# A dense SwiGLU on two 64-row halves of the TensorE array instead of the whole array

## What is computed

```python
def swiglu(h, w_gate, w_up, w_down):
    return (jax.nn.silu(h @ w_gate) * (h @ w_up)) @ w_down

for layer in range(2):
    h = rms_norm(x, norm_mix_g[layer])
    x = x + (even_mixer if layer == 0 else odd_mixer)(h, ...)
    h = rms_norm(x, norm_ffn_g[layer])
    x = x + (swiglu if layer == 0 else moe_swiglu)(h, ...)   # dense: 1024 -> 3584 -> 1024
return rms_norm(x, norm_final_g)
```

## Time and profile before

| | |
|---|---|
| three timed runs | 1423.88, 1424.10, 1425.11 us |
| median | 1424.1 us |
| span of the profiled execution | 1422.2 us |
| own time of the profiled execution | not among the numbers shown; its span is 1.9 us below the median |
| dense feed-forward in the profile | from 128.97 us to about 362.5 us, 233.5 us |
| TensorE busy in the profile | 1394.8 us, 98% |

### The profile page before, as it was taken

One profiled execution on the slowest core, in us unless ns is written; L12 is line 12 of the kernel. 1 busy time (PEld: TensorE's weight loads), 2 busy tenths in 40 slices (PEclk: granted clock), 3 DMA queues, 4 the chain that ended last, 5 costly groups with the idle time before them and its releaser, 6 DMA issues.

```text
span 1422.2 us, 33237 instructions
## 1 busy us (share of the span) xinstructions
PE 1394.8 (98%) x15137; PEld 833.4 (59%) x15137; DVE 441.0 (31%) x748; ACT 328.8 (23%) x528; POOL 29.7 (2%) x42
## 2 busy tenths in 40 slices
PE   6999999999999999999999999999999999999997
PEld 6987888888899853453453353353354354344344
DVE  4656655655686742101101101101101101101102
ACT  4645545445566531000000000000000000000001
POOL 2000000000012100000000000000000000000000
PEclk9999999999999999999999999999999999999998
DMA  9734555556443489999999999999999999999980
GB/s 296 252 119 146 195 177 194 191 180 198 149 120 140 148 332 326 401 419 389 391 418 387 392 417 389 394 415 393 388 414 400 392 405 402 393 402 408 393 332 32
DMA packets 133041, 438.42 MB, mean 308 GB/s; under 512 B 10690, under 2 KB 64160, under 8 KB 116512
## 3 DMA queue, kind: packets, MB, share of 16 engines
q1 hardware_dynamic: 131824, 433.26, 80.1%
q0 software_dynamic: 1072, 2.98, 0.7%
HBM read 435.16 MB, written 1.05 MB: 307 GB/s over the span
## 4 chain that ended last, share of the span: by engine, by line
PE 95%; DVE 3%; DMA 1%; issue 0%; ACT 0%; POOL 0%; SPq 0%; DVEq 0%
PE bank L1366 41%; PE bank L1387 20%; PE bank L1131 6%; PE bank L881 6%; PE bank L883 6%; PE bank L882 6%; PE bank L1132 4%; PE bank L1134 1%; PE bank L1415 1%; PE bank L1435 1%; DMA raw<-in_ev_w_in 1%; DVE arena L2142 0%; PE bank L1003 0%; PE bank L1049 0%; POOL arena L1849 0%
## 5 line engine op out<-in xcount | busy, mean ns | idle before, releaser
L1366 PE MATMUL bank<-ring,arena 128*32 128x512 f32 (+1 forms) x6144 | 583.5, 540 | 0.0
L1366 PEld LDWEIGHTS bank<-ring,arena 128*32 128x32 f32 x6144 | 197.7, 110 | 365.2 <-issue 362.5
L1387 PE MATMUL bank<-ring,arena 128*32 128x256 f32 x5376 | 291.5, 379 | 0.0
L1387 PEld LDWEIGHTS bank<-ring,arena 128*32 128x32 f32 x5376 | 175.1, 110 | 116.7 <-issue 3.1
L679 DVE TENSOR_TENSOR low<-raw,high 128x2048 fp32r<-128x2048 f32 x73 | 167.3, 2294 | 85.1 <-ACT high L674 84.9
L674 ACT ACTIVATE high<-raw 128x2048 fp32r<-128x2048 f32 x73 | 139.3, 1910 | 55.8 <-PE bank L883 44.1
L1131 PE MATMUL bank<-ht_both,high 128*128 128x512 f32 x392 | 140.5, 398 | 0.6 <-DVE ht_both L1901 0.6
L2413 DVE TENSOR_TENSOR expert_rows<-expert_rows,bank 128x512 f32<-128x512 f32 (+1 forms) x48 | 29.8, 621 | 344.3 <-issue 217.3
L1788 ACT ACTIVATE expert_rows<-bank 128x512 f32<-128x512 f32 (+1 forms) x48 | 25.9, 544 | 422.9 <-PE bank L1366 422.9
L1132 PE MATMUL bank<-ht_both,low 128*128 128x256 f32 x448 | 116.8, 281 | 0.0
L1799 ACT ACTIVATE y_h<-bank 128x256 fp32r<-128x256 f32 x24 | 9.2, 383 | 403.9 <-PE bank L1387 403.9
(11 more groups left out here) (316 smaller groups left out, 1206.8 us busy)
## 6 DMA issues: line engine op xcount, KB each, us to landing
ring<-in_moe_w_down SPq DMA_DIRECT2D x112, 1024.0 KB, 8.4
ring<-in_moe_w_gate SPq DMA_DIRECT2D x64, 1024.0 KB, 9.1
ring<-in_moe_w_up SPq DMA_DIRECT2D x64, 1024.0 KB, 8.6
ring<-in_moe_w_gate SPq DMA_DIRECT2D x64, 768.0 KB, 5.9
ring<-in_moe_w_up SPq DMA_DIRECT2D x64, 768.0 KB, 6.6
raw<-in_ffn_w_gate SPq DMA_DIRECT2D x14, 1024.0 KB, 5.0
raw<-in_ffn_w_up SPq DMA_DIRECT2D x14, 1024.0 KB, 5.0
raw<-in_ffn_w_down SPq DMA_DIRECT2D x14, 1024.0 KB, 5.0
```

Source lines behind the costliest of these rows:

```text
L1366: ins = mm(ps(use)[q * GRP:(q + 1) * GRP, 0:width], rows[:, k, r * GRP:(r + 1) * GRP], weights[:, q, :, :], start=k == 0, stop=k == DK - 1)
L1387: ins = mm(ps(use)[q * GRP:(q + 1) * GRP, 0:DN], m_act_t[:, r, first + c, :], ring[:, at + c * DM + q * DN:at + c * DM + (q + 1) * DN], st ...
```

## The change

The order of pieces becomes g, u of half chunk s, then the down piece of half chunk s - 1 (for s = 1 to 11); the last three down pieces stand at the end. Every matmul of a gate, up or down piece (but the last two down pieces) is cut into two of 64 contraction rows, one on rows 0 to 63 of the array and one on rows 64 to 127, issued one after the other into different banks. A gate or up piece is worked in two phases. In the first, the upper rows go to group 2h and the lower rows to group 2h + 1; in the second they are swapped, so that each bank gets the whole sum. The phases run g, u, g, u, and the second waits for the end of the first of its piece (`tile_step`). All three products go into the same 256 columns of a bank. ScalarE applies Silu directly from the gate bank, VectorE multiplies it with the up bank; the copies of second halves and the additions are gone. A down piece has four turns over pairs of quarters, (0, 2), (1, 3), (2, 0), (3, 1).

```diff
-for _c in range(NCH + 1):
-    if _c < NCH:
-        FFN_ORDER += [("g", _c, 0), ("u", _c, 0), ("g", _c, 1), ("u", _c, 1)]
-    if _c:
-        FFN_ORDER += [("d", _c - 1, 0), ("d", _c - 1, 1)]
+for _s, _half in enumerate(FFN_HALVES):
+    FFN_ORDER += [("g", *_half), ("u", *_half)]
+    if 1 <= _s < len(FFN_HALVES) - 2:
+        FFN_ORDER.append(("d", *FFN_HALVES[_s - 1]))
+FFN_ORDER += [("d", *_half) for _half in FFN_HALVES[-3:]]
...
+            def gate_up_phase(n, second):
+                kind, c, h = FFN_ORDER[n]
+                wh, wl = piece(high, N_FFN + n, DK), piece(low, N_FFN + n, DK)
+                chunks = (2 * h + 1, 2 * h) if second else (2 * h, 2 * h + 1)
+                if not second:
+                    pe.wait_ge(*split_done(N_FFN + n))
+                    for j in chunks:
+                        open_bank(pe, (kind, c, j))
+                else:
+                    tiles.wait(first_phase[n])
+                for k in range(DK):
+                    if n == 0 and not second and k % 2 == 0:
+                        pe.wait_ge(*drained(("norm", 1, k // 2)))
+                    for i, (weights, rows) in enumerate(((wh, ht_h), (wh, ht_l), (wl, ht_h))):
+                        begins, ends = (k, i) == (0, 0), (k, i) == (DK - 1, 2)
+                        for part, j in zip(row_tiles, chunks):
+                            cols = slice((j % 2) * P, (j % 2 + 1) * P)
+                            ins = mm(ps((kind, c, j))[:, 0:SEQ], weights[part, k, cols], rows[part, k, :],
+                                     start=begins and not second, stop=ends and second)
...
+            def ffn_down(n):
...
+                for turn, pair in enumerate(((0, 2), (1, 3), (2, 0), (3, 1))):
+                    if turn > 1:
+                        tiles.wait(marks[turn - 2])
+                    for steps in zip(*(down_products(n, q) for q in pair)):
+                        for part, (q, rows, weights) in zip(row_tiles, steps):
+                            last = mm(ps(("fdown", q)), rows[part], weights[part], start=q not in begun, stop=False)
...
-            def second_halves(kind, c, h):
...
             def silu_pair(c, h):
...
+                    act.wait_ge(*filled(use))
                     if (c, h) != (0, 0):
+                        before = FFN_HALVES[FFN_HALVES.index((c, h)) - 1]
+                        act.wait_ge(*drained(("u", before[0], 2 * before[1] + j % 2)))
+                    fn(f_silu[:, j % 2, :], ps(use)[:, 0:SEQ], ACT.Silu).then_inc(drain_sem(use), 1)
...
-            def gate_sums(c, h):
...
             def gated_pair(c, h):
                 for j in (2 * h, 2 * h + 1):
                     use = ("u", c, j)
+                    dve.wait_ge(*filled(use))
+                    dve.wait_ge(*drained(("g", c, j)))
+                    V.tensor_tensor(f_v[:, j % 2, :], ps(use)[:, 0:SEQ], f_silu[:, j % 2, :],
+                                    ALU.mult).then_inc(drain_sem(use), 1)
...
+            for n in range(SPLITS, FFN_PIECES):
+                kind, c, h = FFN_ORDER[n - SPLITS]
+                if kind == "u":
+                    gated_pair(c, h)
+                low_parts(N_FFN + n)
                 if kind == "u":
                     act_low_pair(c, h)
```

More of the change, by code:

```diff
@@ L1116, in _ @@
             transposes_of_norm(1)
[L1118 to L1136, removed]
@@ L1155, in _ @@
[L1155 to L1159, removed]
-                    last.then_inc(ffn_piece_used, 1)
[L1161 to L1171, removed]
+            tiles = Steps(pe, tile_step)
@@ new lines, in _ @@
+            first_phase = {}
+            def gate_up_phase(n, second):
[17 more added lines that the diff above has]
+                                     start=begins and not second, stop=ends and second)
+                            if ends and second:
+                                ins.then_inc(fill_sem((kind, c, j)), 1)
+                if not second:
+                    first_phase[n] = tiles.mark(ins)
@@ new lines, in down_products @@
+            def down_products(n, q):
+                _, c, h = FFN_ORDER[n]
+                wh, wl = piece(high, N_FFN + n, 2), piece(low, N_FFN + n, 2)
+                t, cols = q // 2, slice(q % 2 * 512, q % 2 * 512 + 512)
+                tokens = slice(t * P, (t + 1) * P)
+                for k in range(2):
+                    a = (c % 2) * 4 + 2 * h + k
+                    for rows, weights in ((f_act_h, wh), (f_act_l, wh), (f_act_h, wl)):
+                        yield q, rows[:, a, tokens], weights[:, k, cols]
@@ new lines, in ffn_down_last @@
+            def ffn_down_last(n, quarters):
+                down_ready(n)
+                for q in quarters:
+                    products = list(down_products(n, q))
+                    for i, (_, rows, weights) in enumerate(products):
+                        last = mm(ps(("fdown", q)), rows, weights, start=False,
+                                  stop=n == FFN_PIECES - 1 and i == len(products) - 1)
+                    if n == FFN_PIECES - 1:
+                        last.then_inc(fill_sem(("fdown", q)), 1)
+                if n == FFN_PIECES - 2 and quarters[-1] == 3:
+                    last.then_inc(ffn_piece_used, 1)
```

94 lines of the change are left out of this document (43 added, 51 removed).

## The result

| | before | changed |
|---|---|---|
| timed runs, median | 1425.08 us (1423.88 to 1426.40, 5 runs) | 1430.0 us (1429.25 to 1432.13, 5 runs) |
| ratio | | 1.0039, 95% interval 1.0027 to 1.0051 |
| span of the profiled execution | 1422.2 us | 1430.3 us |

The changed kernel is slower by 0.4%: 5.6 us by the ratio, 4.9 by the medians. That is the time of rival C of the prediction almost to the microsecond, and the upper end of the range.

The account below looks back on a forecast made before the run. TensorE, busy 98% of the span, was taken as the bound. Gate and up -3.6, down 0, tilings +0.2, waits +1.8 gave -1.6 us: span 1420.6, median 1422.5 us, with 1410.5 to 1430 for 8 in 10.

Parts of the forecast that it names:

- rival C: Gate and up: a full load per 256 columns, 64 rows behaving like 128, 0.120 us a pair, slower, 1429.5 us; chance 21%.
- the likeliest case: Whole kernel: pairs at 0.1148 us plus waits make the stage 1.6 us shorter, 1422.5 us; chance 50%.
- price of a pair: Gate and up: two side-by-side 256-column matmuls on halves take 0.1148 us, 1344 times, 3.6 us less than now.
- down, 288 pairs: Down pieces: pairs of 512 columns on halves keep 0.229 us each, so no change.
- changes of tiling: Stage start and before the last two down pieces: going into another tiling costs about 0.1 us, twice, 0.2 us.
- (a): Stage start: the first up piece is needed at 131.7 but ready at 132.8, so TensorE waits 1.0 us.
- (b): Between half chunks 0 and 1: no down piece covers the Silus, splits and product, so TensorE waits 0.3 to 0.4 us.
- (c): Between half chunks 12 and 13: the same queue of work makes TensorE wait 0.4 us.
- Case B: Gate, up and down: halves stream at or near the clock, 1407.4 us in full, 1413.4 half way; chance 22%.
- Loads behind matmuls: TensorE: by the trace, loads already overlap matmuls on the same rows; only some nanoseconds per load can go.
- D: Every half chunk: Silu, split and product late for the gate by some 0.8 us, 13 times, +10 us, 1433; chance 5%.
- The wait of TensorE on its own first phase: Second phases of gate, up and down: the awaited work ended 2.8 us earlier (down 1.4), so it costs nothing.

Follow-up runs that it names:

- second profile: The changed kernel measured and profiled once more, with nothing altered: 1429.8 us, profiled span 1428.1 us.
- first_whole: The changed kernel with only its first half chunk (gate and up pieces) on the whole array, halves afterwards: 1428.08 us, ratio 1.0031 to the kernel before.
- bench: The changed kernel with 24 settings of test matmuls (tiling, columns, load width) run ahead of the feed-forward: 1538.25 us, only distances between starts read.
- whole_array: The changed kernel with its order and evacuation, but every matmul on all 128 rows, 256 columns per load in gate and up: 1428.04 us, ratio 1.0021.
- three_loads: The kernel before, with each 512-column gate or up matmul cut into two of 256 columns, each with its own load: 1429.34 us, ratio 1.0028.
- grouped: The kernel before, with each group's eight 512-column matmuls first, then its eight of 256: 1422.82 us, ratio 0.9994; repeated, 1423.31 us, 0.9996.
- phases_in_turn: The changed kernel with phases in order g, g, u, u, so each second phase waits for the one directly before: 1438.46 us, ratio 1.010.

## Why the prediction was wrong

Forecast 1422.5, measured 1430.0; the likeliest case had the wrong sign. Of the 7.5 us between them 6.6 are the stage, forecast 1.6 us shorter and measured 5.0 longer; most of the rest is the kernel before, whose median was 1424.1 when I forecast and 1425.08 beside the result. The steps, in its order, with the second profile:

| step | forecast, us | measured, us |
|---|---|---|
| gate, up: price of a pair, 1344 times | 0.1148, -3.6 | 0.120, +3.4 |
| down, 288 pairs | 0.229, 0 | 0.229, 0 |
| changes of tiling | +0.2 | +0.2 |
| (a) start | +1.0 | +1.0, of it 0.7 by another wait (first_whole) |
| (b) half chunks 0 and 1 | +0.4 | +0.14 |
| (c) half chunks 12 and 13 | +0.4 | +0.14 |
| sum | -1.6 | +4.9, stage measured +5.0 |

**The step that failed is the price of a pair.** I took it from `combine` "since `combine` shares the tiling", and reasoned "that a tile hides its load better". The difference, 1344 x 0.0052 = 7.0 us, is more than the 6.6 us by which the stage was missed. bench shows that the tiling is not what sets the price of steps of one width, and whole_array and three_loads that the changed kernel's step costs the same without it. The row that shared the operands, the columns and the product was the right one; that it was for 128 rows did not matter. Its value was in the prediction, as the bad end of the range and as case C, whose price, 0.120, and whose +3.4 came out. That its 1429.5 came out to the half microsecond is partly luck: it held 1.8 us of waits where 1.3 were measured, part of them by another cause, and was counted from a median 1.0 us lower. C got 21%.

The trace of before held a better argument than either row, and I passed over it. 256 columns in 0.120 us and 512 in 0.227 are both 0.013 above their columns at 2.4 GHz (0.107 and 0.213). bench adds 384 columns: 0.173, where the columns alone are 0.160. So at the full clock a matmul of 256 to 512 columns with its load costs **columns / 2.4 GHz plus 13 ns**, and more of them for the same columns must cost more. By this alone 448 more are +6.0 us; it was +3.4, because the alternation of 512 and 256 columns that the change removes had cost 0.353 instead of 0.347, and grouped gets part of that back. How much of the 13 ns is the load and how much the matmul itself is not shown, since no run has one without the other: with 32 or 8 weight columns per load the whole array still took 0.118 and 0.117 in bench, with 8 it took 0.112 in the earlier trace rows. Below 256 columns the form does not hold: bench's first steps of 128 took 0.11 us at the full clock, not 0.067. The Trainium skill, page "TensorE: Matmul & The Clock Gate", section "Back-to-back issue gap", has the same form with 2.5 ns in place of 13, for a matmul without a budget for its load; the runs give 120, 173 and 227 ns, the page's formula 109, 163 and 216. Case B, streaming near the clock, had this small constant for support, and falls.

**Loads behind matmuls.** The prediction weighed the rule of the Trainium skill, page "TensorE: Matmul & The Clock Gate", section "The mechanism", that a load overlaps a running matmul only on another row group, and set the trace against it. The runs side with the trace: with loads on the rows of the running matmul (whole_array) and with loads that could alternate between halves the step is 0.120 us, shorter than one load's record of 0.19.

**The waits.** (a) came out in size and only partly in cause. I followed the split of the up piece and missed that a phase opens two banks, while the second was still the norm's. A step that is moved takes all its waits along, and I did not go through the one in `open_bank`. The wait forecast from 131.7 to 132.8 shrank to 0.3, since the stage began 0.7 late and its steps took 0.120. (b) is seen at 143.56 in the second profile:

```profile
143.38 0.28 PE L1142 MATMUL bank<-ht_both,low 64*128 64x256 f32 x2
143.56 0.50 PE L1142 MATMUL bank<-ht_both,high 64*128 64x256 f32 x4
143.88 0.31 PE L1142 MATMUL bank<-ht_both,low 64*128 64x256 f32 x2
```

0.06 and 0.08 us over the pace. Both (b) and (c) have the forecast place and a third of the size. D did not happen: no other phase is late, and the forecast price of a down step, 0.229, held. The wait of TensorE on its own first phase costs nothing at a distance of 2.88 us, and about 0.3 us at none, as phases_in_turn shows.

**Copies and additions**: nothing gained, as forecast; 40.5 us less work on two engines that nobody waited for. The change of tiling is 0.20 us instead of 0.1, but the first one is not extra: the kernel before too lost about 0.1 in its first step after the transposes, so the sum of 0.2 held.

What the experiments point to is the kernel before with the matmuls grouped, 1.0 us shorter in its profiles and not told from the kernel before by its medians. A version that beats it was not found.

## What to carry to other kernels

Count matmuls and their loads as well as columns. When TensorE is the bound, a change that keeps the columns and cuts them into more matmuls, each with its load, pays for each (here 0.240 us for two of 256 columns, 0.227 for one of 512), and one that widens the matmul behind a load earns it back. Price an unseen form by the row that shares its operand widths, and not by the one that shares its tiling or its look; if two rows disagree and nothing explains why, give the case that each stands for its share. And when a step is moved or doubled, go through every semaphore that it waits for, the opening of a bank too.

## What the hardware showed that was not expected

- **Steps of 128 moving columns were no faster than steps of 256.** At a granted clock of 0.50 (1.2 GHz), steps of only 128 moving columns took 0.213 us (first row of bench above), exactly as long as 256 columns. 128 columns at 1.2 GHz are 0.107. At the full clock, in bench's first steps, they took 0.11 us, against 0.120 for 256. That the load of 128 weight columns sets this pace is my reading and not shown: no setting had 128 moving columns behind a smaller load.
- **At half clock the 13 ns are gone.** 256 columns took 0.213 us in bench and in the earlier trace rows, the columns alone; at full clock 0.120, not 0.107. The full clock gives 1.78 times the pace, not 2.
- **The clock fell while TensorE issued without a gap.** Granted clock in bench, as its steps of 128 columns began:

```profile
127.00:129.00 2.00, 0.13 (x2) 1.00 0.45 176
...
130.00:131.00 1.00, 1.00 (x8) 0.56 0.00 0
131.00:132.00 1.00, 1.00 (x6) 0.50 0.06 16
```

  TensorE had been nearly idle until about 129.5. The first steps ran at 0.11 us, those from 130.1 us on at 0.213, and the clock was back near 151 us, while TensorE was busy for 20.74 of the 21 us from 130 to 151.
- **`combine`'s pace** of 0.1134 us for four quarters, in some of its items, was met in no other setting with 128 weight columns. With 32 weight columns halves and quarters have 0.114 and the whole array 0.118. What makes it so was not found.
